# One-hot tables of a top-k routing moved from VectorE to ScalarE, with other edits in two further stages

## The chip, the cores and the metric

The program runs on 1 core of one Trainium2 chip. The metric is the device time of one execution in microseconds. The kernel before takes 4494.52 us (median of 3 runs, 4492.57 to 4501.29).

Engines: TensorE (PE; its weight loads are PEld), VectorE (DVE), ScalarE (ACT), GpSimd (POOL) and SyncE (SP), which here only issues DMAs. Each has its own queue of instructions, in order; they wait for one another by semaphores.

## The reference

Two layers run over 640 tokens (128 of a prompt, 512 of a latent), width 1024. Each has a mixer (layer 0: a state-space scan and a Fourier mix; layer 1: a gated long convolution) and then a product-key mixture of experts. What the change touches:

```python
def peer(h, layer, P):                       # T = 640, 8 heads, 128 keys per side, top 16
    q = (x @ P['peer_wq'][layer]).astype(F32).reshape(T, PEER_HEADS, 2, PEER_DK // 2)
    s1 = jnp.einsum('thd,hnd->thn', q[:, :, 0], P['peer_k1'][layer].astype(F32))
    s2 = jnp.einsum('thd,hnd->thn', q[:, :, 1], P['peer_k2'][layer].astype(F32))
    v1, i1 = lax.top_k(s1, PEER_TOPK)
    v2, i2 = lax.top_k(s2, PEER_TOPK)
    cand = (v1[..., :, None] + v2[..., None, :]).reshape(T, PEER_HEADS, n_cand)
    cidx = (i1[..., :, None] * N_KEYS + i2[..., None, :]).reshape(T, PEER_HEADS, n_cand)
    best, pos = lax.top_k(cand, PEER_TOPK)
    idx = jnp.take_along_axis(cidx, pos, axis=-1)
    gates = jax.nn.softmax(best, axis=-1).astype(h.dtype)
    ...
def long_conv(u, h_f, h_b, skip):
    taps = jnp.concatenate([h_f, jnp.zeros((1, D), F32), h_b[:0:-1]], axis=0)
    uf = jnp.fft.rfft(u, n=2 * L, axis=1)
    tf = jnp.fft.rfft(taps, axis=0)
    y = jnp.fft.irfft(uf * tf[None], n=2 * L, axis=1)[:, :L]
    return y + u * skip
```

## The kernel before

The program is a row of stages. Each is one block in which all engines run their own lists, and the next begins when all have ended. In order: the prologue (tables of the modulation, the spectra of the long convolution's filters), `norm_modulate`, `lora_and_fourier_inputs`, the scan of layer 0, then for each layer `combine`, `peer_route`, `peer_dense_gates`, `peer_experts` and `combine` again; between the layers' experts stand `hyena_inputs`, `hyena_spectra` and `hyena_back`. The change touches four of them.

**Routing (`peer_route`, L463 to L670), once per layer.** The 640 tokens are TT = 5 tiles of 128 tokens on the partitions. For a tile t, TensorE makes the queries of 16 sides (8 heads with 2 sides each): eight matmuls of 128x128 per side (L498) into one of two banks, and one matmul with the keys (L507), 1 side behind. In the trace each of these matmuls leaves two records. ScalarE copies each query to `qT` (L543), again two buffers, and after every four sides their scores to `sc` (L549), which holds two tiles. TensorE starts a side only when the query two before it has been copied.

VectorE searches each side's 128 scores for the 16 largest with their places (`top16`: L433 to L443, two rounds of MAX8 and two of FIND_INDEX8, one MATCH_REPLACE8). In tile 0 it does so in four calls of 4 sides; later all 16 sides in one call, when the tile's last scores are copied. It keeps the places as floats in `idxf` (L622), finishes the previous tile's gates (`normalize`, L602 to L607), forms candidates: the first WIDE = 4 values of side 0 with all 16 of side 1, the other 12 with the first NARROW = 4, 112 in all (L627, L630), and searches these with `top16` (in the timeline the rows whose output is `best`). Then, by small steps that wait for each other (L634 to L643), it turns the place of each winner into a pair `ab` of ranks, one for each side, and writes the one-hot table `eq` [side, winner, rank] by two comparisons with 0 to 15 (L647, 2048 elements each).

GpSimd multiplies these with the places `idxf` (L582), sums over the 16 ranks by halving (L586, L587) and has the key numbers in `sel`; for the first NSP = 2 tiles it also forms the expert's row number (L590 to L592). For the last tile VectorE does the same itself (`decode_last`, L659 to L665). ScalarE takes the exponential for the gates of tile t-1 (L553) after the copies of tile t. TensorE turns `sel` over for tiles 2 to 4 (L525) and ScalarE copies it (L562).

ScalarE's order is fixed by the loop at L565 to L571: copies of t, exponential of t-1, columns of t-2.

**Spectra (`hyena_spectra`, L2427 to L2550).** The input's transform times the filters' spectra. Five pieces: four of the latent (two frequency tiles, two halves of the width) and the context. TensorE makes the even and the odd part (L2465); ScalarE copies the even one (L2480); VectorE forms sum and difference (L2490, L2494) and the complex products (L2501 to L2514); GpSimd combines them (L2541 to L2548). The context comes last, on VectorE alone (L2526 to L2531). The filters' spectra (`taps`) come from DRAM, 20 loads (L2454).

**Prologue.** ScalarE stores these spectra in 20 pieces (`gates<-yT`, L2917) and at its end waits until all have landed (L2929, L2930). Next comes `norm_modulate` (ScalarE from L126) and then `lora_and_fourier_inputs`, whose SyncE list ends by waiting for the modulation's stores (L1123, L1124).

## Time and profile before

| what | us |
|---|---|
| median of 3 runs | 4494.52 |
| profiled execution | 4496.04 |
| its span | 4494.0 |
| TensorE busy in the span | 3936.4 (88%) |
| VectorE busy | 3576.6 (80%) |
| GpSimd busy | 1951.6 (43%) |
| ScalarE busy | 1480.8 (33%) |
| mean granted TensorE clock | 0.942 |
| routing of layer 0, first matmul to the last `sel` | 1059.90 to 1288.27 |

A row of a timeline has its start, its duration, the engine, the line, the operation, output <- inputs, shapes and how many instructions were merged; in brackets the idle time before it and what ended it. A duration contains the latency of the instruction, so the next one can start before it is over. `PEq L60` as releaser means the start of a new stage. The granted clock is in parts of 2.4 GHz; 0.5 is 1.2 GHz.

### The profile page before, as it was taken

The page shows a single profiled execution, that of the slowest core. Times are in us where ns is not written, and L with a number is a line of the kernel's source. Part 1 is how long each engine was busy: PE and PEld are TensorE (multiplying, and loading weights), DVE is VectorE, ACT ScalarE, POOL GpSimd, SP SyncE. Part 2 cuts the span into 40 slices and gives each one's busy share as a digit, 9 for nine tenths or more (in the row PEclk, how much of TensorE's full clock was granted, in tenths as well). Part 3 has the DMA queues.
Part 4 walks back from the last instruction along what each step waited for, and adds up shares of the span by engine and source line. Part 5 has one row for each costly group of instructions (what it writes and reads, how often), then busy time and mean ns, then how long its engine had stood idle before and what let it go on. Part 6 is the DMA issues. An engine that isn't in the chain of part 4 may idle for free. (4 is left out here: it accounts for less than half of the span.)

```text
span 4494.0 us, 79924 instructions
## 1 busy us (share of the span) xinstructions
PE 3936.4 (88%) x29354; PEld 3269.9 (73%) x29354; DVE 3576.6 (80%) x7332; ACT 1480.8 (33%) x2779; POOL 1951.6 (43%) x1687
## 2 busy tenths in 40 slices
PE   7789999878947999999999489689379999999994
PEld 2356666647936899999999387369368999999994
DVE  4346666635997899999999865558988999999998
ACT  1134444422235333333333222022363333333332
POOL 0011111111467566666666400214585666666665
PEclk8899999989979999999999699899799999999997
DMA  9610000030017999999999322200079999999995
GB/s 355 259 67 19 19 19 19 15 117 38 1 28 247 385 407 400 407 405 401 391 398 395 147 97 85 104 38 2 0 219 385 406 396 407 405 407 390 394 397 228
DMA packets 394136, 1044.93 MB, mean 233 GB/s; under 512 B 37367, under 2 KB 168695, under 8 KB 391672
## 3 DMA queue, kind: packets, MB, share of 16 engines
q0 software_dynamic: 147456, 536.94, 30.3%
q1 hardware_dynamic: 219448, 488.74, 29.2%
q10 hardware_dynamic: 27008, 16.25, 1.2%
q8 instruction: 142, 2.33, 0.2%
q14 instruction: 82, 0.67, 0.0%
HBM read 986.26 MB, written 55.54 MB: 232 GB/s over the span
## 5 line engine op out<-in xcount | busy, mean ns | idle before, releaser
L894 PE MATMUL bank<-h_parts,u_parts 128*128 128x384 f32 x6144 | 1118.7, 337 | 38.8 <-DVE u_parts L989 36.5
L894 PEld LDWEIGHTS bank<-h_parts,u_parts 128*128 128x128 f32 x6144 | 1083.3, 189 | 61.0 <-issue 36.9
L904 PE MATMUL bank<-v_parts,gg_parts 128*128 128x512 f32 x4608 | 1101.8, 392 | 9.2 <-DVE v_parts L1009 9.2
L904 PEld LDWEIGHTS bank<-v_parts,gg_parts 128*128 128x128 f32 x4608 | 863.7, 188 | 184.2 <-issue 12.2
L872 POOL DMA_INDIRECT late<-in_peer_v,rows_idx x512 | 618.5, 1208 | 198.6 <-issue 150.3
L978 DVE SCALAR_TENSOR_TENSOR late<-late,yT 128x1024 f32<-128x1024 f32 x512 | 659.9, 1290 | 34.0 <-DMA late<-in_peer_v,rows_idx 19.5
L864 POOL DMA_INDIRECT late<-in_u_rows,rows_idx x256 | 348.1, 1360 | 303.4 <-DVE yT L972 293.2
L945 ACT ACTIVATE gg_parts<-late 128x384 fp32r<-128x384 f32 x256 | 133.7, 522 | 1034.1 <-DVE late L999 1028.7
L968 DVE TENSOR_TENSOR u_parts<-hT,u_parts 128x1024 fp32r<-128x1024 f32 x256 | 311.2, 1216 | 44.4 <-ACT u_parts L942 44.4
L498 PE MATMUL bank<-hT,late 128*128 128x128 f32 x2560 | 315.8, 278 | 8.7 <-PEq L60 8.7
L1009 DVE TENSOR_TENSOR v_parts<-yT,v_parts 128x1024 fp32r<-128x1024 f32 x256 | 311.2, 1216 | 0.0
L972 DVE CUSTOM_DVE_ANT_0 late<-late,rows_h 128x1024 f32<-128x1024 f32 x256 | 310.1, 1211 | 0.0
L498 PEld LDWEIGHTS bank<-hT,late 128*128 128x128 f32 x2560 | 303.1, 195 | 9.5 <-issue 9.5
L710 POOL TENSOR_SCALAR yT<-iota,selT 128x128 f32<-128x128 f32 x384 | 253.3, 678 | 67.4 <-POOLq L60 67.4
L864 POOL DMA_INDIRECT hT<-in_u_rows,rows_idx x128 | 212.8, 1663 | 155.8 <-DVE yT L972 125.2
L942 ACT ACTIVATE u_parts<-hT 128x1024 fp32r<-128x1024 f32 x256 | 269.6, 1053 | 12.4 <-DMA hT<-in_peer_u 12.4
L947 ACT ACTIVATE v_parts<-yT 128x1024 fp32r<-128x1024 f32 x256 | 268.5, 1049 | 0.0
L725 PE MATMUL bank<-yT 128*128 128x128 f32 x1536 | 221.2, 289 | 40.7 <-POOL yT L710 31.5
L725 PEld LDWEIGHTS bank<-yT 128*128 128x128 f32 x1536 | 188.9, 194 | 73.4 <-DVE yT L700 73.4
L864 POOL DMA_INDIRECT u_rows<-in_u_rows,rows_idx x128 | 135.6, 1059 | 229.6 <-DVE yT L972 214.5
L1354 POOL TENSOR_TENSOR work<-work,lmask 128x256 f32<-128x256 f32 x150 | 116.3, 778 | 204.8 <-ACT work L1739 103.0
L700 DVE TENSOR_SCALAR yT<-iota,selT 128x128 f32<-128x128 f32 x672 | 203.9, 359 | 0.0
(380 smaller groups left out, 5658.7 us busy)
## 6 DMA issues: line engine op xcount, KB each, us to landing
yT<-in_peer_v SPq DMA_DIRECT2D x256, 512.0 KB, 6.5
hT<-in_peer_u SPq DMA_DIRECT2D x256, 512.0 KB, 8.1
w_modt<-in_w_mod SPq DMA_DIRECT2D x24, 2048.0 KB, 10.6
late<-gates SPq DMA_DIRECT2D x168, 192.0 KB, 7.8
late<-in_peer_wq SPq DMA_DIRECT2D x32, 512.0 KB, 12.2
gates<-late SPq DMA_DIRECT2D x2, 8192.0 KB, 30.4
gates<-gates_sb SPq DMA_DIRECT2D x2, 8192.0 KB, 30.5
w_raw<-in_hy_w_in SPq DMA_DIRECT2D x24, 512.0 KB, 3.6
```

The costliest lines, as they stand in the source:

```text
L498: mm = pe.matmul(m.bank[n % 2][:, 0:P], S.wq[:, n, k, :], m.hT[:, k, t * P:(t + 1) * P], start=(k == 0), stop=(k == KD - 1))
L725: mm = pe.matmul(m.bank[u][:, q * P:(q + 1) * P], hot[:, u, 1, q, :], hot[:, u, 0, q, :], start=True, stop=True)
L864: pool.indirect_dma_start(ug[n % GR][:, :], None, m.i["u_rows"], bass.IndirectOffsetOnAxis(ap=R.idx[:, n % 2, n // 2:n // 2 + 1], axis=0)) ...
L872: pool.indirect_dma_start(vg[n % GR][:, :], None, v_table, bass.IndirectOffsetOnAxis(ap=R.idx[:, n % 2, n // 2:n // 2 + 1], axis=0)).then_ ...
L894: mm = pe.matmul(m.bank[j % 2][:, 0:TD], us[:, j % 2, a, k, :], hs[:, b, k, :], start=(k == 0 and i == 0), stop=(k == KD - 1 and i == 2))
L904: mm = pe.matmul(yb[t][c][:, :], gs[:, j, a, t * P:(t + 1) * P], vs[:, j % 2, b, c * BANK:(c + 1) * BANK], start=(first and i == 0), stop= ...
L942: act.activation(us[:, j % 2, 0], u_in[:, (j + 2) % 4], ACT.Copy).then_inc(s["pe_uhi"], 1)
L947: act.activation(vs[:, j % 2, 0], v_in[:, j], ACT.Copy).then_inc(s["pe_vhi"], 1)
L968: dve.tensor_tensor(us[:, slot, 1], u_in[:, raw], us[:, slot, 0].bitcast(F32), ALU.subtract).then_inc(s["pe_ulo"], 1)
L972: dve.tensor_tensor_reduce(ug[q % GR][:, :], ug[q % GR][:, :], R.h[:, q % 2, :], 1.0, 0.0, ALU.mult, ALU.add, sd[:, q:q + 1]).then_inc(s[" ...
L978: dve.scalar_tensor_tensor(R.y[:, q % 2, :], vg[q % GR][:, :], sa[:, q:q + 1], R.y[:, q % 2, :], ALU.mult, ALU.add).then_inc(s["pe_axpy"], 1)
L1009: dve.tensor_tensor(vs[:, j % 2, 1], v_in[:, j], vs[:, j % 2, 0].bitcast(F32), ALU.subtract).then_inc(s["pe_vlo"], 1)
```

## The change

**Routing.**
- The one-hot tables of tiles 0 to 3 are made by ScalarE, in a new function `hits`: for each side 16 activations |rank number - ab| over [128 x 128], then one Relu of 1 minus that, in place, over [128 x 2048]. `hits(t-1)` stands behind the exponential of tile t-1, so after the copies of tile t and before the columns and the copies of tile t+1. The last tile's tables stay on VectorE (in `decode_last`), and use the same `eq`, so they wait for GpSimd to have finished with tile 3.
- `eq` is laid out [side, rank, winner] instead of [side, winner, rank].
- GpSimd multiplies each side as soon as its table is there, but starts the sums of tile t only when VectorE has written the first candidates of tile t+1 (`pk_second`).
- VectorE waits for ScalarE's activations on `ab` before it overwrites it (`pk_away`).
- From tile 1 on the sides are searched in two calls of 8, after the second and after the fourth copy of scores.
- WIDE = 3, so 100 candidates instead of 112.

**Spectra.** GpSimd does nothing here. TensorE makes the whole sum (four matmuls) and the even part; ScalarE copies twice the even part; VectorE gets the difference as that minus the sum, reads the sum from PSUM, and does all combinations. The context comes first, and its taps are loaded in the stage before (`load_taps` into `H.taps`).

**Prologue.** The wait for the spectra's stores moves from ScalarE's end of the prologue to the end of SyncE's list two stages later.

```diff
-WIDE = 4
+WIDE = 3
...
-        eq = buf(ctx, nc, "eq", P, 2, PH * TOPK, TOPK)
+        eq = buf(ctx, nc, "eq", P, 2, TOPK, PH * TOPK)
...
+        def times_index(eng, t, side):
+
+            e = eq[:, side].rearrange("p k (h q) -> p k h q", h=PH)
+            index = idxf[:, t % 2].rearrange("p (h s) k -> p s k h", s=2)[:, side].unsqueeze(3).broadcast_to([P, TOPK, PH, TOPK])
+            return eng.tensor_tensor(e, e, index, ALU.mult)
+
+        def fold(eng, half):
+
+            return eng.tensor_tensor(eq[:, :, 0:half], eq[:, :, 0:half], eq[:, :, half:2 * half], ALU.add)
+
+        def choose(eng, t):
+
+            return eng.tensor_tensor(sel[:, t % 2, 0:2, :], eq[:, :, 0], eq[:, :, 1], ALU.add)
...
+                def hits(t):
+                    act.wait_ge(s["pk_ab"], t + 1)
+                    if t >= 1:
+                        act.wait_ge(s["pk_dec"], t)
+                    for side in range(2):
+                        for k in range(TOPK):
+                            ins = act.activation(eq[:, side, k], ab[:, side], ACT.Abs, scale=-1.0, bias=m.iota[:, k:k + 1])
+                        ins.then_inc(s["pk_away"], 1)
+                        act.wait_ge(s["pk_away"], 2 * t + side + 1)
+                        e = eq[:, side].rearrange("p k q -> p (k q)")
+                        act.activation(e, e, ACT.Relu, scale=-1.0, bias=m.iota[:, 1:2]).then_inc(s["pk_hot"], 1)
+
                 for t in range(TT + 2):
                     if t < TT:
                         copies(t)
                     if 1 <= t <= TT:
                         gates(t - 1)
+                    if 1 <= t < TT:
+                        hits(t - 1)
                     if t >= 2:
...
-                    pool.wait_ge(s["pk_place"], t + 1)
-                    iv = idxf[:, t % 2].rearrange("p (h s) k -> p h s k", s=2)
+                    pool.wait_ge(s["pk_ab"], t + 1)
                     for side in range(2):
-                        e = eq[:, side].rearrange("p (h q) k -> p h q k", h=PH)
-                        ins = pool.tensor_tensor(e, e, iv[:, :, side, :].unsqueeze(2).broadcast_to([P, PH, TOPK, TOPK]), ALU.mult)
+                        pool.wait_ge(s["pk_hot"], 2 * t + side + 1)
+                        ins = times_index(pool, t, side)
                     link(ins)
-                    e = eq[:, :, :, :].rearrange("p s q k -> p (s q) k")
+                    pool.wait_ge(s["pk_second"], t + 2)
                     for half in (8, 4, 2):
-                        link(pool.tensor_tensor(e[:, :, 0:half], e[:, :, 0:half], e[:, :, half:2 * half], ALU.add))
-                    ins = pool.tensor_tensor(sel[:, t % 2, 0:2, :].rearrange("p s q -> p (s q)").unsqueeze(2), e[:, :, 0:1], e[:, :, 1:2], ALU.add)
+                        link(fold(pool, half))
+                    ins = choose(pool, t)
...
-                            sides = range(SIDES)
+                        elif b % 2 == 1:
+                            dve.wait_ge(s["pk_sc"], 4 * t + b + 1)
+                            sides = range(4 * b - 4, 4 * b + 4)
...
+                                      v[:, :, 1, :].unsqueeze(2).broadcast_to(shape), ALU.add).then_inc(s["pk_second"], 1)
...
-                    link(dve.scalar_tensor_tensor(ab[:, 0, :], placef[:, 1, :], float(TOPK - NARROW), placef[:, 0, :], ALU.subtract, ALU.max))
+                    if t >= 1:
+                        dve.wait_ge(s["pk_away"], 2 * t)
+                    link(dve.scalar_tensor_tensor(ab[:, 0, :], placef[:, 1, :], float(WIDE * TOPK // NARROW - WIDE), placef[:, 0, :], ALU.subtract, ALU.max))
...
-                    link(dve.tensor_tensor(ab[:, 1, :], posf[:, :], corner[:, 1, :], ALU.subtract))
-                    if t >= 1:
-                        dve.wait_ge(s["pk_dec"], t)
-                    for side in range(2):
-                        ins = dve.tensor_tensor(eq[:, side], ab[:, side, :].unsqueeze(2).broadcast_to([P, PH * TOPK, TOPK]),
-                                                m.iota[:, 0:TOPK].unsqueeze(1).broadcast_to([P, PH * TOPK, TOPK]), ALU.is_equal)
-                    if t < TT - 1:
-                        ins.then_inc(s["pk_place"], 1)
-                    else:
-                        link(ins)
+                    dve.tensor_tensor(ab[:, 1, :], posf[:, :], corner[:, 1, :], ALU.subtract).then_inc(s["pk_ab"], 1)
...
+                    dve.wait_ge(s["pk_ab"], TT)
+                    dve.wait_ge(s["pk_dec"], t)
                     for side in range(2):
-                        e = eq[:, side].rearrange("p (h q) k -> p h q k", h=PH)
-                        ins = dve.tensor_tensor(e, e, iv[:, :, side, :].unsqueeze(2).broadcast_to([P, PH, TOPK, TOPK]), ALU.mult)
+                        ins = dve.tensor_tensor(eq[:, side], ab[:, side, :].unsqueeze(1).broadcast_to([P, TOPK, PH * TOPK]),
+                                                m.iota[:, 0:TOPK].unsqueeze(2).broadcast_to([P, TOPK, PH * TOPK]), ALU.is_equal)
                     link(ins)
...
                 M.store(sp, 5)
                 M.stored(sp, 4)
                 M.stored(sp, 5)
+                for i, n in enumerate(M.spectra):
+                    sp.wait_ge(M.homes[f"hs_st{i}"], 16 * n)
...
+                load_taps(sp, m, H.taps, 0, H.landed)
...
+def load_taps(sp, m, dst, k, sem):
+
+    for j in range(2):
+        for h in range(2):
+            sp.dma_start(dst[:, j, h * BANK:(h + 1) * BANK].rearrange("p (a t) -> p a t", t=SPEC_W), spectrum_rows(m, k, j, h)).then_inc(sem, 16)
...
+                for k in (1, 3, 2, 4):
+                    load_taps(sp, m, taps[:, k - 1], k, s[f"hs_taps{k}"])
...
+                        mm = pe.matmul(banks(0)[2 * h + j][:, :], H.tab.ctx[:, j, :], H.ut[:, 0, h * BANK:(h + 1) * BANK], start=True, stop=True)
+                    mm.then_inc(s["hs_mm"], 1)
+                for n, (c, kt, h) in enumerate(work):
+                    if n == 0:
+                        continue
+                    if n >= 2:
+                        pe.wait_ge(s["hs_free"], n)
+                    for j in range(2):
+                        for i in range(2):
+                            mm = pe.matmul(banks(n)[2 + j][:, :], H.tab.lat[:, i, j, kt * P:(kt + 1) * P], H.ut[:, 1 + i, h * BANK:(h + 1) * BANK], start=(i == 0), stop=(i == 1))
+                    mm.then_inc(s["hs_half"], 1)
+                    for j in range(2):
+                        for t in range(4):
+                            mm = pe.matmul(banks(n)[j][:, :], H.tab.lat[:, t, j, kt * P:(kt + 1) * P], H.ut[:, 1 + t, h * BANK:(h + 1) * BANK], start=(t == 0), stop=(t == 3))
+                    mm.then_inc(s["hs_mm"], 1)
...
+                for n in range(1, len(work)):
+                    act.wait_ge(s["hs_half"], n)
+                    if n >= 2:
+                        act.wait_ge(s["hs_free"], n + 1)
                     for j in range(2):
-                        ins = act.activation(even[:, j], banks(n)[2 * j][:, :], ACT.Copy)
+                        ins = act.activation(ev[:, j], banks(n)[2 + j][:, :], ACT.Copy, scale=2.0)
...
+                dve.wait_ge(H.landed, 16 * 4)
...
+                    one, other = taps[:, kt], taps[:, 2 + kt]
+                    both = banks(n)[0:2]
+                    dve.wait_ge(s["hs_mm"], n + 2)
...
+                    dve.wait_ge(s["hs_even"], n)
                     for j in range(2):
-                        ins = dve.tensor_tensor(pa[:, j], plus[:, j], taps[:, 1 + kt, j, sl], ALU.mult)
+                        dve.tensor_tensor(mn[:, j], ev[:, j], both[j][:, :], ALU.subtract)
+                    for j in range(2):
+                        dve.tensor_tensor(pa[:, j], both[j][:, :], one[:, j, sl], ALU.mult)
+                    for j in range(2):
+                        ins = dve.tensor_tensor(pc[:, j], both[j][:, :], one[:, 1 - j, sl], ALU.mult)
+                    ins.then_inc(s["hs_free"], 1)
+                    dve.wait_ge(s["hs_free"], n + 2)
+                    for j in range(2):
+                        dve.tensor_tensor(pb[:, j], mn[:, j], other[:, j, sl], ALU.mult)
+                    for j in range(2):
+                        dve.tensor_tensor(mn[:, j], mn[:, j], other[:, 1 - j, sl], ALU.mult)
+                    dve.tensor_tensor(pa[:, 0], pa[:, 0], pa[:, 1], ALU.subtract)
+                    link(dve.tensor_tensor(pc[:, 0], pc[:, 0], pc[:, 1], ALU.add))
+                    dve.tensor_tensor(pb[:, 0], pb[:, 0], pb[:, 1], ALU.subtract)
+                    link(dve.tensor_tensor(mn[:, 0], mn[:, 0], mn[:, 1], ALU.add))
+                    for y, a, b in ((H.y[0], pa, pb), (H.y[1], pc, mn)):
+                        dve.tensor_tensor(y[:, 1 + kt, sl], a[:, 0], b[:, 0], ALU.add)
+                        ins = dve.tensor_tensor(y[:, 3 + kt, sl], a[:, 0], b[:, 0], ALU.subtract)
                     link(ins)
...
-            @block.gpsimd
-            def _(pool):
-                for n, (kt, h) in enumerate(work):
-                    sl = slice(h * BANK, (h + 1) * BANK)
-                    pool.wait_ge(s["hs_b"], n + 1)
-                    if n >= 1:
-                        pool.wait_ge(s["hs_pair"], n)
-                    pool.tensor_tensor(yb[:, 0], pb[:, 0], pb[:, 1], ALU.subtract)
-                    pool.tensor_tensor(yb[:, 1], minus[:, 0], minus[:, 1], ALU.add).then_inc(s["hs_yb"], 1)
-                    pool.wait_ge(s["hs_yb"], n + 1)
-                    pool.wait_ge(s["hs_a"], n + 1)
-                    for j in range(2):
-                        pool.tensor_tensor(H.y[j][:, 1 + kt, sl], ya[:, j], yb[:, j], ALU.add)
-                    for j in range(2):
-                        ins = pool.tensor_tensor(H.y[j][:, 3 + kt, sl], ya[:, j], yb[:, j], ALU.subtract)
-                    ins.then_inc(s["hs_pair"], 1)
-                pool.wait_ge(s["hs_pair"], N)
...
+            H.taps = buf(middle, nc, "taps_ctx", P, 2, D)
+            H.landed = sems(middle, nc, "hi_taps")["hi_taps"]
...
+        self.homes = sems(ctx, nc, *[f"hs_st{i}" for i in range(4)])
...
-                for i in range(RING):
-                    act.wait_ge(s[f"hs_st{i}"], 16 * stored(len(work), i))
+                M.spectra = [stored(len(work), i) for i in range(RING)]
```

On ScalarE in layer 0's routing, from the last score copy of tile 1 (`yT` is the memory of `sc`) to the first copies of tile 2, before:

```order
L549 ACTIVATE yT<-bank 128x512
L553 ACT_TABLE_LOAD
L553 ACTIVATE gatex<-gatex 128x128
L543 ACTIVATE qT<-bank 128x128 x5
L549 ACTIVATE yT<-bank 128x512
L543 ACTIVATE qT<-bank 128x128 x4
```

and now (`eq<-ab` are the 16 activations of a side, `eq<-eq` its Relu):

```order
L563 ACTIVATE yT<-bank 128x512
L567 ACT_TABLE_LOAD
L567 ACTIVATE gatex<-gatex 128x128
L585 ACTIVATE eq<-ab,iota 128x128 x16
L589 ACTIVATE eq<-eq,iota 128x2048
L585 ACTIVATE eq<-ab,iota 128x128 x16
L589 ACTIVATE eq<-eq,iota 128x2048
L557 ACTIVATE qT<-bank 128x128 x5
L563 ACTIVATE yT<-bank 128x512
```

Between the exponential and the next copies, which stood side by side, there are now 34 activations. The same stands after tiles 2, 3 and 4.

On VectorE in the spectra, one latent piece before (`plus` and `minus` are sum and difference, `pa` and `pb` products):

```order
L2490 TENSOR_TENSOR plus<-even,bank 128x512 x2
L2494 TENSOR_TENSOR minus<-even,bank 128x512 x2
L2501 TENSOR_TENSOR pa<-plus,taps 128x512 x2
L2504 TENSOR_TENSOR plus<-plus,taps 128x512 x2
L2506 TENSOR_TENSOR pb<-minus,taps 128x512 x2
L2509 TENSOR_TENSOR minus<-minus,taps 128x512 x2
L2513 TENSOR_TENSOR ya<-pa 128x512
L2514 TENSOR_TENSOR ya<-plus 128x512
```

and now (`bank` is PSUM, `pc` a third product, `hT` and `y_sin` hold the result):

```order
L2540 TENSOR_TENSOR minus<-even,bank 128x512 x2
L2542 TENSOR_TENSOR pa<-bank,taps 128x512 x2
L2544 TENSOR_TENSOR pc<-bank,taps 128x512 x2
L2548 TENSOR_TENSOR pb<-minus,taps 128x512 x2
L2550 TENSOR_TENSOR minus<-minus,taps 128x512 x2
L2551 TENSOR_TENSOR pa<-pa 128x512
L2552 TENSOR_TENSOR pc<-pc 128x512
L2553 TENSOR_TENSOR pb<-pb 128x512
L2554 TENSOR_TENSOR minus<-minus 128x512
L2556 TENSOR_TENSOR hT<-pa,pb 128x512
L2557 TENSOR_TENSOR hT<-pa,pb 128x512
L2556 TENSOR_TENSOR y_sin<-pc,minus 128x512
L2557 TENSOR_TENSOR y_sin<-pc,minus 128x512
```

One piece has 18 instructions instead of 14 (x2 counts two), six of which read the sum from PSUM, and the last four write what GpSimd wrote.

## Rows read from the trace of the kernel before

**Rows 1.** The timeline of VectorE, layer 0, tile 2 (start us, us, ...).

```profile
1166.07 3.18 DVE L433 MAX8 vals<-yT 128x8 f32<-128x128 f32 x16
...
1185.29 0.29 DVE L622 CAST idxf<-idx 128x256 f32<-128x256 uint32 x1
...
1198.96 4.49 DVE L647 TENSOR_TENSOR eq<-ab,iota 128x2048 f32<-128x2048 f32 x2
```

**Rows 2.** The timeline of VectorE, last tile, layer 0, then layer 1.

```profile
1273.56 4.49 DVE L647 TENSOR_TENSOR eq<-ab,iota 128x2048 f32<-128x2048 f32 x2
...
1278.85 4.49 DVE L659 TENSOR_TENSOR eq<-eq,idxf 128x2048 f32<-128x2048 f32 x2
...
1287.68 0.59 DVE L665 TENSOR_TENSOR sel<-eq 128x256 f32<-128x256 f32 x1
...
3213.22 0.59 DVE L665 TENSOR_TENSOR sel<-eq 128x256 f32<-128x256 f32 x1
```

**Rows 3.** The timeline of TensorE in layer 0's routing; then a window.

```profile
1059.90 6.62 PE L498 MATMUL bank<-hT,late 128*128 128x128 f32 x32 [4.21 <-PEq L60]
...
1127.92 3.74 PE L498 MATMUL bank<-hT,late 128*128 128x128 f32 x32
1131.49 0.39 PE L507 MATMUL bank<-keys,qT 128*128 128x128 f32 x2
...
1059.90:1066.40 6.50, 6.50 (x33) 6.50 (x34) 0.00 (x0) 0.28 (x1) 0.00 (x0) 0.55 0.01 3
```

**Rows 4.** The timeline of ScalarE in layer 0's routing.

```profile
1128.73 1.28 ACT L553 ACT_TABLE_LOAD   x1
...
1160.69 0.60 ACT L549 ACTIVATE yT<-bank 128x512 f32<-128x512 f32 x1 [0.58 <-PE bank L507]
...
1234.28 0.31 ACT L553 ACTIVATE gatex<-gatex 128x128 f32<-128x128 f32 x1 [5.91 <-DVE gatex L634]
```

**Rows 5.** The timeline of ScalarE, then groups by line and shape.

```profile
256.02 0.37 ACT L1676 ACTIVATE sw<-bank,pcol 128x128 f32<-128x128 f32 x1 [0.73 <-PE bank L1364]
256.29 0.36 ACT L1676 ACTIVATE sa<-bank,pcol 128x128 f32<-128x128 f32 x1
...
L738 ACT ACTIVATE key_away<-iota,first_neg 128x128 f32<-128x128 f32 x96 | 37.7, 392 | 0.1
...
L2912 ACT ACTIVATE yT<-dec,tn 128x2048 f32<-128x2048 f32 x5 | 9.9, 1999 | 18.3 <-DVE pm L2964 18.2
```

**Rows 6.** The timeline of GpSimd, layer 0, tile 2.

```profile
1203.53 9.03 POOL L582 TENSOR_TENSOR eq<-eq,idxf 128x2048 f32<-128x2048 f32 x2 [18.18 <-DVE eq L647]
...
1220.76 0.63 POOL L587 TENSOR_TENSOR sel<-eq 128x256 f32<-128x256 f32 x1
```

**Rows 7.** The timelines of VectorE, then TensorE, in the spectra.

```profile
2802.14 1.28 DVE L2490 TENSOR_TENSOR plus<-even,bank 128x512 f32<-128x512 f32 x2
...
2804.66 3.38 DVE L2501 TENSOR_TENSOR pa<-plus,taps 128x512 f32<-128x512 f32 x2
...
2815.14 1.29 DVE L2490 TENSOR_TENSOR plus<-even,bank 128x512 f32<-128x512 f32 x2
...
2848.23 1.29 DVE L2526 TENSOR_TENSOR pa<-bank,taps 128x512 f32<-128x512 f32 x2
...
2851.35 0.68 DVE L2531 TENSOR_TENSOR y_sin<-plus 128x512 f32<-128x512 f32 x1
...
2781.54 30.27 PE L2465 MATMUL bank<-ut,dft 128*128 128x512 f32 x64 [2.65 <-PEq L60]
2817.68 6.65 PE L2470 MATMUL bank<-ut,dft 128*128 128x512 f32 x8 [5.87 <-DVE minus L2494]
```

**Rows 8.** The timeline of ScalarE, end of prologue and of routing.

```profile
117.27 2.88 ACTq L2917 DMA_DIRECT2D gates<-yT  x4
128.75 1.28 ACT L127 ACT_TABLE_LOAD   x1 [10.89 <-PEq L60]
...
1292.26 0.37 ACT L731 ACTIVATE first_neg<-selT 128x96 f32<-128x96 f32 x1 [2.49 <-PEq L60]
```

104 lines of the change are left out of this document (26 added, 78 removed).

## The prediction

> **What bounds the kernel now.** I read the table of engines over time first: one core, four stretches that the change touches (the end of the prologue, the routing of each of the two layers, the spectra of the second layer), everything else untouched and strictly behind them, since each stage begins after a barrier. So each stretch counts in full, and in each the question is which engine comes last.
>
> In the routing the timeline of VectorE shows it. From tile 2 on it never rests (no idle time stands in its rows): the searches over the 16 sides begin at 1166.07, idxf follows at 1185.29, and the tables (eq) at 1198.96. So a tile is 19.2 us of searches, 13.7 of candidates, positions and small steps, and 4.4 of one-hot tables (two, started 4.49 less 0.1 of overlap with what follows), 37.3 in all [rows 1]. The last tile's tables begin at 1273.56, and its products and sums follow on the same engine, so `sel` is complete at 1288.27 [rows 2]. TensorE is close behind: from 1127.92, when its groups of tile 2 begin, to the end of that tile's fourth score copy at 1161.29 it takes 33.4 us [rows 3, 4]. ScalarE copies TensorE's results, and has time: before the exponential of tile 3 it waits 5.91 us for VectorE [rows 4]. What the reader must see there is the coupling: TensorE has two banks for queries, so it can run two groups (x32 records, 3.6 us) past the last copy, and no further. ScalarE's copies are hardly any work, but TensorE stands still without them.
>
> **The routing's edits, ScalarE first.** Per tile 0 to 3 it gets 32 Abs of 128x128 (bias from a column, written to SBUF), two Relu of 128x2048 and two waits for its own results. They stand between the copies of tile t+1 and the copies of tile t+2, so they are a block H in which nothing is copied. Abs of this form in the dense gates takes 392 ns [rows 5], and two neighbouring activations with a bias column start 0.27 us apart though each lasts 0.37: an overlap of 0.10 [rows 5]. So 0.295 us each, 9.4 us for 32. A 128x2048 activation with one column operand takes 2.00 us [rows 5], two make 4.0. With two drains of about 0.1, H = 13.6 us. Bounds: 11.0 if Abs were as dense as 0.22 (0.31 for the shorter exponential less 0.10 [rows 4]), 16.9 if nothing overlapped. I take 13.6, by the nearest row.
>
> The Trainium skill (ScalarE: Activation LUTs, "What ACT_TABLE_LOAD costs") gives 280 ns + 0.833 ns per element with a bias operand and an overlap of 93 ns: that would be 0.294 per Abs and an estimate of H of 13.4. No run so far shows 16 Abs in a row.
>
> Now TensorE. It does the first two groups of tile t+2 (until 1131.49 in tile 2 of the trace [rows 3]) and then stands until the block is over, about 12 us (1128.7 + 1.5 + 13.6 is 1143.8). From there to the end of the tile's fourth score copy the trace has 29.8 us (1131.49 to 1161.29 [rows 3, 4]); this stretch now begins only when H is over, plus 0.3 for the first copy. And the clock: after 4.21 us of idleness the 32 records from 1059.90 take 6.62 us where the same 32 take 3.74 at 1127.92, and the granted clock in that stretch (the third number from the row's end) is 0.55, which is 1.2 instead of 2.4 GHz for most of it [rows 3]. Twelve us of standing still are more than 4.2, so I add 2.9 us to each restart. Bounds: 0 and 3.6 (a whole pair of groups at half speed). One round of ScalarE is then 0.3 + 29.8 + 2.9 = 33.0 for the copies, 0.2 for the exponential, H, and about 1.1 for columns: 48 us against 37.3 before. VectorE isn't the bound any more.
>
> The chain in layer 0: copies of tile 1 end at 1128.7, unchanged; table load and exponential 1.5 [rows 4]; four times H, 54.4; three rounds of copies, 99.0; exponentials and columns between them 2.8. ScalarE ends the tables of tile 3 at 1286.4. GpSimd then multiplies the second side, 4.5, and sums, 8.8 (9.03 for two products; 17.9 from 1203.53 to the end of `sel` at 1221.39 [rows 6]): 1299.7. VectorE's last tile waits for that (it uses the same eq) and then makes tables, products and sums itself, 13.95 us (14.71 from 1273.56 to 1288.27 [rows 2], less 0.76 for the normalisation, which stands before 1278.85, when the products begin): 1313.7. Against 1288.27: +25.4 us. Layer 1 has the same rows 1925.54 us later (`sel` from 3213.22) [rows 2], so +50.8 for both.
>
> VectorE's new wait (pk_away, before it overwrites ab) ends some 12 us after a tile's last score copy; VectorE gets there 20.7 after it: no cost.
>
> VectorE's own edits lie under this. Without the tables its tile is 4.4 shorter; WIDE = 3 leaves 100 of 112 candidates, between 0 and 1.5 us (12/112 of 13.7), I take 0.6; halves of 8 sides add four waits, between 0 and 1.0, I take 0.5. It needs 9.9 + 13.1 us behind the last scores of tile 4 (1272.5), so is ready at 1296.3 with the normalisation, 3 us before GpSimd. That is the cover: nothing of it reaches the end. If H shrank so far that VectorE led again, the 4.5 saved per tile would count. The new wait of GpSimd (sums only once VectorE has written tile t+1's first candidates) holds up only GpSimd, behind which stand its own sums; its pk_dec still comes before ScalarE's next block, which waits for it, so no one waits but at the tail above. The change of loop order in eq leaves element counts alone; cost 0, bounds plus or minus 2 us per layer.
>
> **Spectra.** VectorE ends this stage at 2852.03 [rows 7]. A round of sums, differences and products took 13.0 us (2802.14 to 2815.14), with 14 instructions. GpSimd's adds go; VectorE now has 18 per round. The six in a round of the context take 3.8 with their waits (2848.23 to 2852.03) [rows 7], 0.633 each, so 18 take 11.4. The context moves to the front: two rounds of 3.8 from about 2785.1 (four half-speed records of TensorE, 0.85 each, after 2781.54). The first latent round needs 8 + 24 records of TensorE, about six of them at the lower clock: 6 x 0.85 + 26 x 0.43 = 16.3, so 2798.1. Then 4 x 11.4: 2843.7, a gain of 8.3. (0.85 is 6.65 us over 8 records after 5.87 us of idleness, 0.43 half of it [rows 7].) TensorE's 24 x 0.43 = 10.3 per round stay under 11.4. Bounds: 0.69 per instruction (no overlap) gives a gain of 4, 0.60 (1.29 for two less 0.69) gives 10.7. Four taps loads moved to SyncE's queue of the stage before cost nothing: it has been done long before TensorE there.
>
> What speaks for the gain is that two products from 2804.66, beside GpSimd's adds, take 3.38 us instead of 1.29 [rows 7]. The Trainium skill (SBUF — State Buffer, "Who interferes with whom") says why: a VectorE instruction with two SBUF inputs and a GpSimd one that reads SBUF exclude each other for a whole instruction. These rows agree.
>
> **Prologue.** ScalarE issues its last stores until 120.15; the next stage begins at 128.75 [rows 8]. A boundary without such a wait leaves ScalarE idle for 2.49 us, as before 1292.26 [rows 8]. Awaiting the stores 90 us later gives 128.75 - 122.64 = 6.1. Lower bound 0, if the next stage's weights, asked for 6.1 us earlier too, then come late; nothing in these rows says so, and I take 6.1.
>
> **Sum.** +50.8 - 8.3 - 6.1 = +36.4. The profiled execution took 4496.04 (span 4494.0 and 2.04 around it), 1.5 above the median of the three timed runs, 4494.52. On the median: 4531 us. A measurement here tells about 0.2%, 9 us, from no change.
>
> **Rivals.**
> - The clock holds through TensorE's pauses. For it: no row shows 12 us of idleness here; against it the stretch after 4.21 us. Three rounds lose 2.9 less, in two layers: -17.4, 4514.
> - GpSimd and VectorE lock each other out. GpSimd's products of 4.5 us now fall in the middle of a tile, beside VectorE's casts and additions, and at the tail beside its nine small linked steps. By the pair at 2804.66 a step waits for the rest of the other's instruction. In mid-tile VectorE has slack; at the tail one product's length, 4.5 per layer, so 4540. By the rule of the Trainium skill named above (SBUF — State Buffer) it would be so, and the searches, with one SBUF input, would be free.
> - Not slower: the block on ScalarE is short. The place is H, its price counts four times per layer. If Abs cost only its elements (2.00 - 0.39 over 1920 elements is 0.84 ns, 0.107 us for 128 [rows 5]), H would be 7.3, TensorE's pause about 3.5 us and perhaps without a fall of the clock: ScalarE ends at 1252.5, VectorE leads, and a layer ends 5.6 us early; total 4494.5 - 11.2 - 14.4 = 4469. It decides from H = 9.1 us on, where a layer costs 7.2 more and the other gains cancel it (25.4 - 4 x 4.55). Against it: no activation in the trace starts less than 0.22 after its neighbour, which gives H = 11.0 and with the lower clock 4510.
> - The prologue's wait was covered by something else (its gain is 0): 4537.
>
> **Chances.** Forecast 0.62, clock holds 0.12, lock 0.12, prologue without gain 0.04, short block 0.10, half of it faster and half within the 9 us. Sum: faster 0.05, same 0.05, slower 0.90. The range: from H = 11.0 with a slow restart less what the spectra could add (4505) up to H near 15 with the lock (4546).
>
> **What the changed profile would show.** ScalarE's 16 Abs at a pitch of about 0.295 and a Relu of 2.0 us; TensorE idle about 12 us after two groups of tiles 2, 3 and 4, each restart with 32 records over 6 us instead of 3.7; in the routing 1060 to 1290 a stretch longer by 25 us, with VectorE's idle time before tile 3 and 4 from ScalarE's score copies; GpSimd, not VectorE, releasing the last tile's tables; the spectra's VectorE rows done 8 us earlier after their start; the stage after the prologue 6 us earlier. I'd be wrong if VectorE still ran without a pause at 33 us per tile, which would mean that ScalarE's block fits into TensorE's two groups of lead.

## The result and the profile after

The kernel after takes 4526.49 us (median of 4 runs, 4524.36 to 4531.5) against 4493.55 for the kernel before (4 runs): a ratio of 1.0071, 95% interval [1.0054, 1.0089], so 0.5 to 0.9% slower, 33 us. The forecast was 4531 in a range from 4505 to 4546. The profiled execution took 4531.5 us with a span of 4529.7. One of the seven executions of spectra_only below took 17218 us at a mean granted clock of 0.225 and is left out of its interval; the median of the other six is 4481.1.

TensorE in the routing of layer 0, the timeline (columns as in [rows 3]) and then two windows (the third number from a row's end is the granted clock, as a share of 2.4 GHz):

```profile
1056.46 6.35 PE L512 MATMUL bank<-hT,late 128*128 128x128 f32 x32 [4.21 <-PEq L60]
...
1124.21 3.74 PE L512 MATMUL bank<-hT,late 128*128 128x128 f32 x32
...
1140.26 0.79 PE L521 MATMUL bank<-keys,qT 128*128 128x128 f32 x2 [12.31 <-ACT qT L557]
...
1127.80:1140.20 12.40, 0.15 (x2) 0.00 (x0) 12.19 (x61) 12.34 (x32) 3.90 (x2) 0.59 0.00 1
1140.20:1146.50 6.30, 6.24 (x41) 6.24 (x42) 6.20 (x49) 0.73 (x4) 6.22 (x2) 0.72 0.01 3
```

This is the pause that [rows 3] do not have: two groups of the new tile (3.74 us), then 12.31 us of nothing until ScalarE's copy of a query (`qT`). In the 6.3 us behind it the granted clock is 0.72, so it was still at 1.2 GHz for part of them, though less long than behind the 4.21 us of idle time in [rows 3], where the stretch has 0.55.

ScalarE in the same stretch:

```profile
1126.54 4.76 ACT L585 ACTIVATE eq<-ab,iota 128x128 f32<-128x128 f32 x16
1131.33 2.00 ACT L589 ACTIVATE eq<-eq,iota 128x2048 f32<-128x2048 f32 x1
...
1138.04 2.00 ACT L589 ACTIVATE eq<-eq,iota 128x2048 f32<-128x2048 f32 x1
...
1171.88 4.77 ACT L585 ACTIVATE eq<-ab,iota 128x128 f32<-128x128 f32 x16
...
1218.90 4.77 ACT L585 ACTIVATE eq<-ab,iota 128x128 f32<-128x128 f32 x16
...
1266.28 4.76 ACT L585 ACTIVATE eq<-ab,iota 128x128 f32<-128x128 f32 x16
...
1277.79 2.00 ACT L589 ACTIVATE eq<-eq,iota 128x2048 f32<-128x2048 f32 x1
```

The block lasts from 1126.54 to 1140.04, 13.5 us, and TensorE stands for 12.31 of them. It comes back after 45.3, 47.0 and 47.4 us, where VectorE's tile of 37.3 set the pace before [rows 1]. GpSimd and VectorE at the last tile of layer 0, to be read against [rows 2] and [rows 6]:

```profile
1279.86 3.82 POOL L490 TENSOR_TENSOR eq<-eq,idxf 128x2048 f32<-128x2048 f32 x1 [2.82 <-ACT eq L589]
1283.76 8.33 POOL L494 TENSOR_TENSOR eq<-eq 128x2048 f32<-128x2048 f32 x3
1292.17 0.72 POOL L498 TENSOR_TENSOR sel<-eq 128x256 f32<-128x256 f32 x1
```

```profile
1266.29 1.64 DVE L433 MAX8 vals<-yT 128x8 f32<-128x128 f32 x8 [4.92 <-ACT yT L563]
...
1276.17 1.02 DVE L649 CAST idxf<-idx 128x256 f32<-128x256 uint32 x1
...
1288.47 2.36 DVE L664 CAST posf<-pos_u 128x128 f32<-128x128 uint32 x1
...
1291.00 1.23 DVE L666 CAST placef<-place 128x256 f32<-128x256 uint32 x1
...
1294.63 4.49 DVE L679 TENSOR_TENSOR eq<-ab,iota 128x2048 f32<-128x2048 f32 x2
...
1307.99 0.43 DVE L498 TENSOR_TENSOR sel<-eq 128x256 f32<-128x256 f32 x1
```

GpSimd is done at 1292.89 and VectorE begins its tables at 1294.63, with no idle time in front: the last to arrive is VectorE, by 1.7 us. `sel` is complete at 1308.42, 251.96 us after the first score matmul, where the kernel before needed 228.37 [rows 2, 3]: +23.6. Layer 1 has +23.6 too (251.56 us from 2999.05 to 3250.61, and 227.98 before).

The spectra, VectorE and then TensorE (compare [rows 7]), and ScalarE at the end of the prologue (compare [rows 8]):

```profile
2820.95 1.28 DVE L2540 TENSOR_TENSOR minus<-even,bank 128x512 f32<-128x512 f32 x2 [5.15 <-PE bank L2497]
...
2832.26 1.28 DVE L2540 TENSOR_TENSOR minus<-even,bank 128x512 f32<-128x512 f32 x2
...
2865.47 0.69 DVE L2557 TENSOR_TENSOR y_sin<-pc,minus 128x512 f32<-128x512 f32 x1
```

```profile
2804.40 6.16 PE L2484 MATMUL bank<-ut,dft 128*128 128x512 f32 x8 [2.64 <-PEq L60]
2867.57 0.77 PE L2582 MATMUL bank<-idft,hT 128*128 128x128 f32 x2 [15.81 <-PEq L60]
```

```profile
114.07 3.05 ACTq L2928 DMA_DIRECT2D gates<-yT  x4
119.34 1.28 ACT L127 ACT_TABLE_LOAD   x1 [4.68 <-PEq L60]
```

A round of the spectra is 11.3 us (2820.95 to 2832.26) instead of 13.0, the last one ends 61.8 us after TensorE's first matmul of the stage (2866.16) and not 70.5. Behind the prologue ScalarE is idle for 4.68 us and not 10.89.

### The profile page after: what moved, and what is told of

It reads as the page before. It is cut to its first block and busy times, and to the rows that moved or that the text cites. A ratio compares the mean times of both kernels' runs of the same rounds, so it can differ in the third digit from the quotient of the medians.

```text
span 4529.7 us, 80280 instructions
## 1 busy us (share of the span) xinstructions
PE 3960.4 (87%) x29386; PEld 3292.0 (73%) x29386; DVE 3574.3 (79%) x7332; ACT 1587.7 (35%) x3051; POOL 1906.4 (42%) x1663
## 5 line engine op out<-in xcount | busy, mean ns | idle before, releaser
L1001 DVE SCALAR_TENSOR_TENSOR late<-late,yT 128x1024 f32<-128x1024 f32 x512 | 660.4, 1291 | 33.4 <-DMA late<-in_peer_v,rows_idx 18.9
L512 PE MATMUL bank<-hT,late 128*128 128x128 f32 x2560 | 326.3, 284 | 8.4 <-PEq L60 8.4
L512 PEld LDWEIGHTS bank<-hT,late 128*128 128x128 f32 x2560 | 314.3, 201 | 9.2 <-issue 9.2
L490 POOL TENSOR_TENSOR eq<-eq,idxf 128x2048 f32<-128x2048 f32 x16 | 61.1, 3822 | 374.0 <-ACT eq L589 374.0
L312 POOL TENSOR_TENSOR x<-x,gb 128x1024 f32<-128x1024 f32 x8 | 18.8, 2351 | 456.2 <-ACT x L262 456.2
```

What stands on the lines that cost most here:

```text
L512: mm = pe.matmul(m.bank[n % 2][:, 0:P], S.wq[:, n, k, :], m.hT[:, k, t * P:(t + 1) * P], start=(k == 0), stop=(k == KD - 1))
L1001: dve.scalar_tensor_tensor(R.y[:, q % 2, :], vg[q % GR][:, :], sa[:, q:q + 1], R.y[:, q % 2, :], ALU.mult, ALU.add).then_inc(s["pe_axpy"], 1)
```

## The experiments

Eleven more runs were made; before_again and spread_again repeat a kernel. Times are medians, ratios are to the kernel before on the same chip. "Routing" is the stretch in layer 0 from the first score matmul to the first matmul of the dense gates, "scan" the one from the scan stage's first matmul to the mixer's output projection, each in one profiled execution.

```
kernel          us        ratio, 95% interval        routing   scan
before          4493.55   1                          234.0     719.6
before_again    4491.44   0.9999 [0.9990, 1.0008]    234.1     718.3
after           4526.49   1.0071 [1.0054, 1.0089]    257.7     725.3
route_only      4546.05   1.0117 [1.0102, 1.0131]    258.3     718.4
prologue_only   4488.63   0.9990 [0.9982, 0.9999]    233.8     718.4
spectra_only    4481.86   0.9975 [0.9963, 0.9986]    233.7     720.9
double_abs      4607.54   one run                    294.8     724.3
warm_pe         4514.40   1.0044 [1.0028, 1.0059]    251.4     724.4
tables_only     4537.08   1.0092 [1.0077, 1.0107]    263.0     721.8
halves_only     4471.02   0.9950 [0.9934, 0.9965]    224.0     718.1
halves_all      4458.28   0.9919 [0.9905, 0.9932]    223.9     719.1
spread          4458.69   0.9918 [0.9901, 0.9935]    223.4     722.5
spread_again    4459.51   0.9911 [0.9898, 0.9925]    223.4     727.4
```

### The parts by themselves: route_only, prologue_only, spectra_only

Each is the kernel before with one part of the diff: the new `peer_route` and `WIDE = 3`; the waits for the spectra stores moved to SyncE at the end; the new spectra stage.

> The kernel before with the new routing alone (tables by ScalarE, sums by GpSimd, searches by half, cut at three); prologue and spectra as before. Theory (the routing alone costs time, because TensorE stops for ScalarE's block of tables): each routing is 23.6 us longer, as in the trace after (251.96 against 228.37), so 4493.5 + 47 = 4541 us. Rival (the parts act together: the earlier starts that prologue and spectra hand on move a weight load into the routing, and the change's cost is partly theirs): routing grows by 15 or less and the time is 4525 or less, and prologue or spectra alone cost time. The dense gates' first work after routing 0 should come 23.6 later than in the kernel before by the theory.

> The kernel before with the waits for the spectra stores moved from ScalarE's queue to the end alone. Theory A (the next stage starts 6 to 9 us sooner and all that follows keeps it): 4484 to 4488 us. Theory B (the scan gives it back: in the trace after, its start is 8.7 sooner and its end only 2.9 sooner, with no edit between): the scan takes about 725 us instead of 720, and the time is 4490 to 4492. Theory C (the scan's length is noise between executions, or comes from another edit): the scan stays within 2 us of what this day's kernel before shows.

> The kernel before with the spectra stage of the kernel after alone (what GpSimd did given to the others). Theory: the stage is 9.15 us shorter, as in the trace after (63.17 against 72.32), and what follows keeps it: about 4484 us. Rival (a transfer or a weight load sets when the next stage starts): the stage ends sooner but the next stage starts as before, and the time is 4493.

Measured: +53.0, -4.4 and -11.2 us, together +37 where the whole change has +33. route_only came 5 us above its expectation of 4541, the other two within 5 us of theirs. The routing's stretch is 24.3 us longer in route_only, 23.7 in the kernel after, so it owes nothing to the other parts. In spectra_only TensorE's first matmul of the spectra and of the next stage stand 62.7 us apart:

```profile
2784.79 5.65 PE L2459 MATMUL bank<-ut,dft 128*128 128x512 f32 x8 [2.65 <-PEq L60]
2847.46 0.77 PE L2557 MATMUL bank<-idft,hT 128*128 128x128 f32 x2 [15.81 <-PEq L60]
```

and prologue_only has ScalarE idle for 4.82 us behind its last copies:

```profile
117.47 1.28 ACT L127 ACT_TABLE_LOAD   x1 [4.82 <-PEq L60]
```

The scan did not give the prologue's gain back there (718.4), so theory B of that run falls, though its time, 4488.6, is just above theory A's. By its interval the part is worth 0.4 to 8 us.

### How much two executions differ: before_again, spread_again

> The kernel before, unchanged, to see how far stages without an edit differ between two executions. If the scan (first instruction to the first combine) takes 719.6 us again within 1, its 5.8 us more in the trace after belong to the change; if it differs by 3 or more, stage lengths of one execution can't be told apart below that size. Time 4493.5 us either way.

> The kernel with the tables in portions once more, beside the one without ScalarE's tables on the same chip: 4458.7 us, within 2.

The untouched scan took 725.3 us in the trace after, 5.8 more than before. One and the same kernel (spread and spread_again) has 722.5 and 727.4, while before and before_again have 719.6 and 718.3. A single execution therefore can't tell differences below 5 us in this stage. Of the seven executions with the new prologue and the new spectra together six lie above all without both (718.1 to 720.9), and halves_all, which has both too, at 719.1. Whether the two together cost the scan a few us stays open.

### Is the block H the price? double_abs

```
+ ins.then_inc(s["pk_twice"], 1)
+ act.wait_ge(s["pk_twice"], 2 * t + side + 1)
+ for k in range(TOPK):            # the same 16 Abs once more
+     ins = act.activation(eq[:, side, k], ab[:, side], ACT.Abs, scale=-1.0, bias=m.iota[:, k:k + 1])
```

> The kernel after with each of the 32 Abs of a block done twice (same result): the block H grows from 13.5 to about 23.2 us. Theory (in tiles 1 to 3 H stands whole in the round, since TensorE waits for its copies, and once more at the end): a round becomes 47.0 + 9.7 = 56.7, the routing 4 x 9.7 = 38.8 longer, twice: 4526.5 + 78 = 4604 us. Rival (VectorE's searches and chain set the round, H only fills their idle time): the round grows by less than 5 us, and the time is under 4560.

ScalarE and TensorE in layer 0, double_abs:

```profile
1186.16 4.77 ACT L585 ACTIVATE eq<-ab,iota 128x128 f32<-128x128 f32 x16
...
1243.33 4.77 ACT L585 ACTIVATE eq<-ab,iota 128x128 f32<-128x128 f32 x16
```

```profile
1154.10 0.80 PE L521 MATMUL bank<-keys,qT 128*128 128x128 f32 x2 [21.93 <-ACT qT L557]
```

The round is 57.2 us, TensorE's pause 21.93, the stretch 37.1 longer (38.8 expected) and the time 4607.5 (4604 expected, one execution). From 13.5 us on, each further us of ScalarE's block is paid nearly four times per routing (37.1 for 9.7), so VectorE does not set the round there. That is not so for the first us of the block, see halves_all below.

### What the clock takes of it: warm_pe

```
+ if t >= 2 and n == 1:
+     pe.wait_ge(s["pk_sc"], 4 * t)
+     for _ in range(48):
+         pe.matmul(m.bank[7][:, 0:P], S.wq[:, 0, 0, :], m.hT[:, 0, t * P:(t + 1) * P], start=True, stop=True)
```

> The kernel after with 48 matmuls more in each of TensorE's pauses of tiles 2 and 3 (results never read), started when the last score copy of the tile before is done, so that the engine works while ScalarE writes its tables. Theory (each restart after a pause costs TensorE's next columns about 2.9 us because the granted clock has fallen to its lower level): the four pauses covered give back up to 2.9 each where clock and not copies bound, 4515 to 4526 us, and the x32 groups right after a pause read 3.7 instead of 6.3. Rival (after a pause the copies by ScalarE bind, not the clock): the groups read less, but the round stays 47.0 us and the time 4526.

The expectation speaks of tiles 2 and 3 and of four pauses; `t >= 2` takes in tile 4 as well, so three pauses per routing are covered, six in all. TensorE, timeline and windows, and ScalarE:

```profile
1145.05 0.49 PE L525 MATMUL bank<-keys,qT 128*128 128x128 f32 x2 [1.59 <-ACT qT L561]
...
1130.00:1144.00 14.00, 13.46 (x121) 13.27 (x119) 13.79 (x70) 13.93 (x36) 3.85 (x1) 1.00 0.01 2
1144.00:1151.00 7.00, 5.95 (x53) 5.95 (x54) 6.86 (x51) 1.72 (x5) 6.01 (x2) 1.00 0.01 2
```

```profile
1131.33 4.77 ACT L589 ACTIVATE eq<-ab,iota 128x128 f32<-128x128 f32 x16
...
1175.04 4.78 ACT L589 ACTIVATE eq<-ab,iota 128x128 f32<-128x128 f32 x16
...
1219.74 4.77 ACT L589 ACTIVATE eq<-ab,iota 128x128 f32<-128x128 f32 x16
```

The granted clock is 1.00 through the pause and behind it, and a round takes 43.7 to 44.7 us instead of 45.3 to 47.4. The last block of layer 0 starts 133.1 us after the first one (at 1264.44), against 139.7 in the kernel after: 2.2 us per pause. The routing's stretch is 6.3 us shorter, so the rival (the round stays 47.0 us) falls. The time is 12.1 us lower, though the two intervals of the table overlap a little. The clock is about 6.5 us of each routing; what is left of the 23.7 is mainly the block's length, less what the halves give back.

### Halves and tables apart: halves_only, tables_only

halves_only is the kernel before with searches by 8 sides from tile 1 on (tile 4 too, though its expectation says 1 to 3) and `WIDE = 3`; tables_only is the kernel after with whole searches and `WIDE = 4`.

```
- elif b == 3:                      (halves_only; tables_only the other way round)
-     dve.wait_ge(s["pk_sc"], 4 * t + 4)
-     sides = range(SIDES)
+ elif b % 2 == 1:
+     dve.wait_ge(s["pk_sc"], 4 * t + b + 1)
+     sides = range(4 * b - 4, 4 * b + 4)
```

> The kernel before with two parts of the change alone: searches of tiles 1 to 3 in two halves of 8 sides, and the candidates cut at three rows instead of four; the tables stay with VectorE and GpSimd. Theory (the kernel before is bound by VectorE's sum of work, and waits there for the scores of a whole tile before the first search): about 9 us per routing come back from VectorE's idle time ahead of tile 1, 4475 us (4468 to 4486). Rival (the idle time only moves to the second half's wait, since the scores of sides 8 to 15 come as late as before): 4493, no change.

> The kernel after with whole searches in place of halves (VectorE waits for all 16 sides of a tile) and the cut at four rows. Theory (in tiles 1 to 3 ScalarE's block sets the round, so the halves give nothing there; at the end of the last tile the second half alone stands behind the last score): one half of a search, 9.9 us by the trace after (1266.29 to 1276.17), more per routing and 0.4 for the wider cut: 4526.5 + 21 = 4547 us, round 47.0. Rival (VectorE's later table input reaches ScalarE's next block): the round grows too, 4560 or more.

Halves and the cut at three, which were not tried apart, take 10.0 us off the stretch and 22.7 off the time. Where they come from stands in the trace of the kernel before, ahead of the search of tile 1:

```profile
1128.75 1.45 DVE L433 MAX8 vals<-yT 128x8 f32<-128x128 f32 x7 [9.89 <-ACT yT L549]
```

In halves_only 0.80 us of it is left, ahead of the second half of tile 1 (1124.34). The prediction looked only from tile 2 on, where VectorE never rested, and did not see these 9.89 us. In tables_only the halves' absence costs only 5.3 us (263.0 against 257.7), not 10.3, and 10.6 in all, not 21. The miss is on VectorE's small steps at the tail. Counted from the copy of the last scores, the cast of `pos_u` comes 8.8 us later in tables_only (30.9 us behind it, and 22.2 in the kernel after), and GpSimd's sums, which wait for the candidates, only 3.6 us later. They are done by then:

```profile
1281.69 8.46 POOL L494 TENSOR_TENSOR eq<-eq 128x2048 f32<-128x2048 f32 x3 [3.56 <-DVE cand L654]
```

```profile
1279.89 0.29 DVE L649 CAST idxf<-idx 128x256 f32<-128x256 uint32 x1
...
1291.60 0.22 DVE L664 CAST posf<-pos_u 128x128 f32<-128x128 uint32 x1
...
1294.20 4.49 DVE L679 TENSOR_TENSOR eq<-ab,iota 128x2048 f32<-128x2048 f32 x2
```

The cast of `pos_u` takes 0.22 us there, and 2.36 in the kernel after, where it falls beside GpSimd's sums. From `idxf` to the last tables VectorE needs 14.3 us here and 18.5 there: the 4.2 us between them are most of what was missing from the expectation.

### The same tables in portions: spread, halves_all

spread does ScalarE's 32 Abs four at a time behind the first eight query copies of two tiles later, so no copy waits for more than a portion and a Relu of half size; only the tables of tile 3 stay one block. halves_all is the kernel after with the tables given back to VectorE.

```
  act.activation(S.qT[:, n % 2], m.bank[n % 2][:, 0:P], ACT.Copy).then_inc(s["ps_qsb"], 1)
+ if t >= 2 and n < 8:
+     part(t - 2, n)                # four Abs; after every second portion a Relu of 128x1024
...
- if 1 <= t < TT:
+ if t == TT - 1:
      hits(t - 1)
```

> The kernel after, with ScalarE's tables of tiles 0 to 2 no longer in one block: they are cut into eight portions of four Abs (a Relu after every second one), one behind each of the first eight query copies of two tiles later; the last tables stay a block. Theory (what costs time is that ScalarE's block holds up the copies for which TensorE waits; the work itself fits beside them): 16 copies at 2.06 take 33 us and 13.5 of tables lie partly between them, the round falls from 47.0 towards 37 to 42, and the time to 4445 to 4500. Rival (ScalarE's sum of work, copies and tables, sets the round whatever the order): the round stays 45 to 47 and the time 4520 to 4526. Second rival (VectorE, with 6.5 us of chain beside GpSimd's products, becomes the bound): round 40 to 44, 4490 to 4510.

> The kernel after with the tables given back to VectorE and GpSimd as in the kernel before; searches by half, the cut at three, prologue and spectra stay as in the kernel after. If the parts add up (halves -22.5, spectra -9.2, prologue -4.4 to -5.9): 4455 to 4458 us. Theory (ScalarE's tables give nothing even where their order costs nothing, since TensorE's columns and the end of the last tile bound the routing in both): the same within 3 us as the kernel with the tables in portions (4458.7). Rival (tables off VectorE are worth something once they stand in portions): 8 us or more slower than that. And: if the scan takes 724 us here too, as in all kernels so far that hold prologue and spectra together, its 5 us more belong to the two together; at 718 to 720 they do not.

TensorE in spread:

```profile
1156.74 3.74 PE L512 MATMUL bank<-hT,late 128*128 128x128 f32 x32
...
1190.18 3.74 PE L512 MATMUL bank<-hT,late 128*128 128x128 f32 x32
```

It has a tile every 33.4 us; from 1125 to 1222 it is busy for 96.7 of 97 us at a clock of 1.00. What the block cost is read from halves_all, the same kernel without ScalarE's tables: 257.7 against 223.9, 33.8 us per routing. (The 23.7 against the kernel before are what is left when the halves' 10.0 are taken off.) That is 2.5 times 13.5 us and not four times: without the block VectorE's tile of 37.3 sets the round and not TensorE's 33.4, so by an estimate from these two numbers the first 4 us of a block cost nothing in a round. In portions the same work costs nothing, 223.4. And since spread keeps the new layout of `eq`, GpSimd's late sums and the wait `pk_away`, none of these is the price. But the tables on ScalarE bring nothing either: 4458.7 with them, 4458.3 without. VectorE is the bound in spread (behind 1124.19 it has no idle time in the stage), as its second rival had it, though at 4459 and not at 4490 to 4510. VectorE, first in spread, then in halves_only, in the same tile, with GpSimd in spread between them:

```profile
1134.08 3.77 DVE L660 CAST idxf<-idx 128x256 f32<-128x256 uint32 x1
...
1148.33 2.21 DVE L672 TENSOR_TENSOR gatex<-best 128x128 f32<-128x128 f32 x1
1150.61 2.37 DVE L675 CAST posf<-pos_u 128x128 f32<-128x128 uint32 x1
...
1153.15 1.24 DVE L677 CAST placef<-place 128x256 f32<-128x256 uint32 x1
...
1176.15 3.23 DVE L660 CAST idxf<-idx 128x256 f32<-128x256 uint32 x1
```

```profile
1133.86 3.84 POOL L490 TENSOR_TENSOR eq<-eq,idxf 128x2048 f32<-128x2048 f32 x1 [99.51 <-ACT eq L594]
...
1145.87 8.37 POOL L494 TENSOR_TENSOR eq<-eq 128x2048 f32<-128x2048 f32 x3
```

```profile
1134.23 0.29 DVE L622 CAST idxf<-idx 128x256 f32<-128x256 uint32 x1
...
1144.99 0.29 DVE L634 TENSOR_TENSOR gatex<-best 128x128 f32<-128x128 f32 x1
1145.34 0.22 DVE L637 CAST posf<-pos_u 128x128 f32<-128x128 uint32 x1
1145.73 0.29 DVE L639 CAST placef<-place 128x256 f32<-128x256 uint32 x1
...
1171.47 0.29 DVE L622 CAST idxf<-idx 128x256 f32<-128x256 uint32 x1
```

Four steps take 9.59 us instead of 1.09, because GpSimd multiplies and sums in the middle of VectorE's tile: the first cast ends at 1137.85, just behind GpSimd's product (1137.70), and the other three lie in its sums (until 1154.24). From `idxf` to `idxf` spread needs 42.1, 36.0 and then 33.2 us, halves_only 37.3 in each (of the later ones, 1208.71 and 1246.07 there). The three tiles together: 111.3 against 111.9. Of the 4.4 us of tables per tile that VectorE was to save, 13.2 in all, 12.6 went into such waits: 9.2 in the first tile, 3.1 in the second, hardly any in the third, where GpSimd's work falls beside searches. The tables of tile 0, saved too, went into waiting for tile 1's scores (4.92 us of idle time ahead of 1124.19). Whether the portions would pay over more tiles was not tried. spread and halves_all beat the kernel before, by 0.6 to 1.0%.

## Why the prediction was right, point by point

**The block H**: right, 13.5 us for 13.6; 16 Abs take 4.76 us and each lasts 0.386 (4 of them take 1.26), so they start 0.292 apart, for 0.295. The formula that the prediction quotes from the Trainium skill (ScalarE: Activation LUTs, "What ACT_TABLE_LOAD costs"), 0.294, agrees. **TensorE's pause**: right, 12.31 for 12. **The restart**: right in kind, with 2.2 us for 2.9; warm_pe is the only run that separates it. The sign "32 records over 6 us" did not come: behind the first pause they take 3.32 and 1.95, behind the second 3.62 and 2.19. ScalarE's tables of tile 3 end 153.3 us after the first block's start where the working had 156.2, and most of the difference is this term (3 x 0.7).

**Who comes last at the tail**: wrong. The prediction had VectorE ready 3 us before GpSimd and called that the cover. VectorE came 1.7 us after it. Its small steps were put at their undisturbed durations, yet ran beside GpSimd's sums: from `idxf` to its tables VectorE needed 18.5 us, where the working had 13.9 (13.1 and the normalisation). GpSimd's own part was as taken, 13.1 us from ScalarE's last table to `sel` for 13.3 (3.82 for a product and not 4.5, but 9.1 for the sums and not 8.8). So the second rival, that the two lock each other out, is true as a mechanism in every tile of the kernel after from tile 1 on, and was wrong in its price (4.5 us per routing, on top of the forecast): its 4.6 us used up the cover first, and 1.7 us were left. The rule of the Trainium skill (SBUF — State Buffer, "Who interferes with whom") names casts and copies beside instructions with two SBUF inputs as those that can contend with GpSimd; the casts of 3.77 and 2.37 us here agree. It lets instructions with one SBUF input go free, and the searches kept their 1.65 us for 8 MAX8 beside GpSimd too (1202.28 in spread). **The tail's own work**: 13.79 us for 13.95.

**The routing as a whole**: +23.6 us for +25.4. GpSimd was done 3.4 us earlier than worked out, 3 of them because ScalarE was, VectorE came 1.7 behind it, and the tail's own work took 0.2 less. double_abs shows that around its true length H counts nearly four times per routing, as the third rival's price had it; that rival itself fell, since H was 13.5 and not 9.1 or less. Its other end, a layer 5.6 us early once VectorE leads, was too small: with the block out of the way (spread, halves_all) a routing is 10 us shorter than before, because the search by halves ends nearly all of the 9.89 us of idle time ahead of tile 1, which the working does not have. It counted halves as a cost of 0.5 us.

**Spectra**: -9.15 us for -8.3; the round is 11.3 us for 11.4. The first latent round begins 16.55 us after TensorE's start, as worked out. Four shorter rounds make 0.4 of the difference, and 0.4 more lies ahead of the next stage. Alone the part gave 11.2 us (6 to 17 by its interval).

**Prologue**: ScalarE's idle time fell by 6.2 us (10.89 to 4.68) for 6.1. The next stage began 9.4 us sooner in the trace, 3 of which stood ahead of the stores already and vary between executions: TensorE's first matmul of that stage is at 122.8 to 131.3 us in the five executions without the edit and at 116.4 to 123.6 in the eight with it. Alone the part gave 4.4 us, so that the fourth rival falls, narrowly.

**Sum**: +33 measured against +36.4. In the profiled executions the routings are 3.6 us shorter than worked out, the spectra 0.9 and the way to `norm_modulate` 3.3, and the scan, which the working left alone, is 5.8 longer; all but the routing's part lies within what single executions differ by. That 4531 came within 5 us is so in part luck: the restart taken too long and VectorE's waits taken at nothing went against each other.

## What to carry to other kernels

Before work is moved to an engine with idle time, look at what that engine feeds: ScalarE was idle for two thirds of the time, but TensorE stood when it did not copy for longer than two groups take (3.7 us), and four blocks of 13.5 us cost 34 us per routing; the same instructions in portions of four, behind copies that TensorE did not need at once, cost nothing. A busy engine's relief must be counted at where its other steps then fall: VectorE gave away 13 us of tables in three tiles and lost nearly all of it to steps that waited beside GpSimd. And take a change's parts apart: searches by halves with the cut at three were worth 22.7 us by themselves, of which the block left 10.6.

## What was unexpected of the hardware

- A cast on VectorE of 128x128 from uint32 to float took 0.22 us alone and 2.36 to 2.38 beside GpSimd's sums, one of 128x256 0.29 and up to 3.77. A shift of 128x128 (TENSOR_SCALAR, uint32) between them kept its 0.21.
- GpSimd's product of 128x2048 took 3.82 us here and half of 9.03 in [rows 6]: the change lays eq out with the 16 table places outermost. The three sums took 8.3 to 8.5 us, and 8.0 to 8.1 in the old layout. That layout was not tried by itself.
- 48 matmuls whose result nobody reads kept TensorE at 2.4 GHz through a pause and made the program 12 us faster (median) than the one without them.
- One stage without an edit, the scan, took 722.5 and 727.4 us in two executions of the same kernel, while their spans, 4459.8 and 4460.2 us, are the same: what a stage loses in one execution others give back.
